# Out-projection of both FFNs as a separate stage of seven Strassen passes over all hidden blocks

## The reference, cut to what matters

```
hf = modulate(rmsnorm(x, norm_w[l, 2]), sh2, sc2)
gate, up = split(hf @ ffn_w_in[l], 2)            # 1024 x 5632
y  = (silu(gate) * up) @ ffn_w_out[l]            # 2816 x 1024, the out-projection
x  = x + g2 * rmsnorm(y, norm_w[l, 3])
```

## Time and profile before

| | |
|---|---|
| runs | 2746.82, 2747.04, 2750.24 us; median 2747.04 |
| profiled execution | 2749.15 us, span 2747.4 us, mean granted clock 0.983 |
| TensorE busy | 2629.4 us, 96%, 12848 matmuls |
| weight loads | 2195.4 us, 80% |
| VectorE | 1691.7 us, 62% |
| GpSimd | 1152.2 us, 42% |
| ScalarE | 966.5 us, 35% |
| DMA | 269 MB, 98 GB/s on average |

### The profile page before, as it was taken

One profiled execution on the slowest core, in us unless ns is written; L12 is line 12 of the kernel. 1 busy time (PEld: TensorE's weight loads), 2 busy tenths in 40 slices (PEclk: granted clock), 3 DMA queues, 4 the chain that ended last, 5 costly groups with the idle time before them and its releaser, 6 DMA issues.

```text
span 2747.4 us, 36296 instructions
## 1 busy us (share of the span) xinstructions
PE 2629.4 (96%) x12848; PEld 2195.4 (80%) x12848; DVE 1691.7 (62%) x2376; ACT 966.5 (35%) x1856; POOL 1152.2 (42%) x788
## 2 busy tenths in 40 slices
PE   7999999999989889999999998999999999999998
PEld 6888788878878678888888877888787888888886
DVE  5378778667756475666656565666436555554556
ACT  5334434443443653233222344111154232223323
POOL 3112332342230036666555641444305665556662
PEclk9999999999999999999999999999999999999999
DMA  6222422432261332112211132332514111111113
GB/s 247 85 70 100 169 108 77 154 128 80 100 227 65 130 123 75 63 62 90 71 61 61 54 139 107 108 107 107 201 52 138 47 59 62 48 46 46 61 46 146
DMA packets 76132, 269.07 MB, mean 98 GB/s; under 512 B 8688, under 2 KB 8688, under 8 KB 72944
## 3 DMA queue, kind: packets, MB, share of 16 engines
q1 hardware_dynamic: 76016, 267.53, 27.1%
HBM read 217.16 MB, written 50.33 MB: 97 GB/s over the span
## 4 chain that ended last, share of the span: by engine, by line
PE 84%; DVE 7%; issue 3%; POOL 3%; ACT 2%; DMA 1%; SPq 0%; POOLq 0%; DVEq 0%; ACTq 0%
PE psum L1189 18%; PE psum L1190 17%; PE psum L1191 17%; PE psum L1720 5%; PE psum L1722 5%; PE psum L1721 5%; PE psum L1386 2%; PE psum L1431 2%; PE psum L1433 2%; PE psum L1432 2%; PE psum L1226 1%; PE psum L1373 1%; PE psum L1246 1%; DVE ada_acc L2581 1%; DVE c_set L2413 1%
## 5 line engine op out<-in xcount | busy, mean ns | idle before, releaser
L1189 PE MATMUL psum<-x_hi,unit 128*128 128x512 f32 x1232 | 484.2, 393 | 5.8 <-DVE x_lo L2413 5.4
L1190 PE MATMUL psum<-x_lo,unit 128*128 128x512 f32 x1232 | 481.5, 391 | 0.0
L1191 PE MATMUL psum<-x_hi,unit 128*128 128x512 f32 x1232 | 481.2, 391 | 0.0
L2413 DVE TENSOR_TENSOR c_set<-c_set,psum 128x512 f32<-128x512 f32 x352 | 233.7, 685 | 354.4 <-PE psum L1191 187.3
L1106 POOL TENSOR_TENSOR unit_sum<-ffn_raw 128x512 f32<-128x512 f32 x200 | 268.2, 1341 | 391.1 <-PE psum L1189 230.2
L2413 DVE TENSOR_TENSOR y<-y,psum 128x512 f32<-128x512 f32 x288 | 193.8, 686 | 159.1 <-PE psum L1722 154.7
L1189 PEld LDWEIGHTS psum<-x_hi,unit 128*128 128x128 f32 x1232 | 232.4, 189 | 61.1 <-ACT c_set L1834 6.2
L1111 POOL TENSOR_TENSOR unit<-unit_sum,unit 128x512 fp32r<-128x512 f32 x200 | 257.6, 1297 | 55.8 <-ACT unit L1834 55.5
L1191 PEld LDWEIGHTS psum<-x_hi,unit 128*128 128x128 f32 x1232 | 232.4, 189 | 48.7
L1190 PEld LDWEIGHTS psum<-x_lo,unit 128*128 128x128 f32 x1232 | 232.4, 189 | 47.6
L1189 PE MATMUL psum<-h_hi,w_hi 128*128 128x512 f32 x624 | 266.3, 427 | 1.3 <-DVE h_lo L2413 1.3
(11 more groups left out here) (303 smaller groups left out, 5290.8 us busy)
## 6 DMA issues: line engine op xcount, KB each, us to landing
ffn_raw<-in_w_ffn_in SPq DMA_DIRECT2D x80, 512.0 KB, 3.5
ffn_raw<-in_w_ffn_out SPq DMA_DIRECT2D x44, 512.0 KB, 4.1
w_raw<-in_w_hgrn_in SPq DMA_DIRECT2D x40, 512.0 KB, 4.7
ada_raw<-in_ada SPq DMA_DIRECT2D x32, 512.0 KB, 3.5
conv_ada_raw<-in_ada SPq DMA_DIRECT2D x32, 512.0 KB, 4.7
units_kept<-stage_unit SPq DMA_DIRECT2D x28, 512.0 KB, 6.1
unit<-units_kept SPq DMA_DIRECT2D x28, 512.0 KB, 4.9
rows_kept<-stage_row SPq DMA_DIRECT2D x12, 1024.0 KB, 8.4
```

The lines of the kernel that those rows point to most:

```text
L1189: begin = pe.matmul(out_ap, hi[:, a:b], rhs_hi, start=first, stop=False)
L1190: pe.matmul(out_ap, hi[:, a:b], rhs_lo, start=False, stop=False)
L1191: return begin, pe.matmul(out_ap, lo[:, a:b], rhs_hi, start=False, stop=last)
L2413: V.tensor_tensor(dst, a, b, op).then_inc(S[sem], 1)
```

## The change

Both FFNs are ordered anew.

- The in-projection runs through all 22 pairs without a matmul of the out-projection between them. `hidden_part` now only multiplies, into one of four fp32 blocks `hid`. VectorE forms five sums of each group's two blocks (`part_sum`, into `part_sums`); SP stores them and two plain halves as seven 128x512 blocks per group in a DRAM tensor `parts_kept` (`parts_store`).
- The low parts of M4 and M3 are made on VectorE (`unit_low`) in place of GpSimd. `ffn_raw` has four slots of one row each.
- The out-projection is a stage after the last pair (`out_products`): seven passes in the order M5, M1, M4, M7, M3, M2, M6, each over the 11 groups, 77 steps. A step loads one kept block (ring of six), splits it (ScalarE `part_high`, VectorE `part_low`), makes the row unit from rows of `ffn_w_out` that lie in SBUF (GpSimd `rows_total` in five passes, ScalarE `row_high`, low part on GpSimd, in these passes on VectorE in every second step), and multiplies: 4 token blocks x 3 matmuls, each token block in a bank of its own that collects the whole pass. Units are in rings of four: what is made for a step may begin when the step three before it has begun.
- After a pass VectorE adds its four banks to the parts of `y` that need them (`out_evac`, 48 operations per FFN), two per step, in steps 3 to 6 of the next pass.
- The last four steps of the last pass run token block by token block. Token blocks 0 to 3 are final after the pass M3; their norms, scalings and turns (8 of 16) are put beside the last two passes, those of blocks 4 to 7 follow the last steps. In the first FFN two convolution panels are loaded and split during the stage.

```
-GROUP_UNITS = 2 * PRODUCTS + 4
+PAIR_UNITS = PRODUCTS * PAIRS
+OUT_KINDS = (M5, M1, M4, M7, M3, M2, M6)
+ROWS_SUMMED = (M1, M4, M7, M3, M6)
+STEPS = PRODUCTS * FFN_GROUPS
+TAIL_GROUPS = 4
+PART_RING, UNIT_RING = 6, 4
...
 # VectorE
-                    tt(up, up, gate, ALU.mult, "hidden_done")
-                    dve.wait_ge(S["hidden_done"], done)
-                    V.tensor_copy(hi[:, cols], up).then_inc(S["hidden_hi_done"], 1)
-                    dve.wait_ge(S["hidden_hi_done"], done)
-                    tt(lo[:, cols], up, hi[:, cols], ALU.subtract, "hidden_ready")
+                    if h is not None:
+                        dve.wait_ge(S["parts_stored"], h * GROUP_STORED + GROUP_STORED * (FFN_GROUPS * f - 1))
+                    tt(hid[e % 4][:, cols_of(half)], up, gate, ALU.mult, "hidden_done")
+                def part_sum(g, k1, j):
+                    dve.wait_ge(S["hidden_done"], g * 4 + (2 * PAIRS * f + 4))
+                    if not (isinstance(g, int) and g + f == 0):
+                        dve.wait_ge(S["parts_stored"], g * GROUP_STORED + GROUP_STORED * FFN_GROUPS * f)
+                    one, other, op = part_terms(OUT_SUMS[j], k1, (k1 + 1) % 4)
+                    tt(part_sums[:, j, :], one, other, op, "part_summed")
...
+                for n in range(2, STEPS):
+                    part_low(n)
+                    if low_by_vector(n):
+                        rows_low(n)
+                    for j in range(len(OUT_SUMS)):
+                        if n == 2 + j // 2:
+                            part_sum(FFN_GROUPS - 1, 0, j)
+                    ...
+                    for m in range(len(EVACS)):
+                        if evac_position(m) == n:
+                            out_evac(m)
+                    if n in EARLY_SCALE:
+                        out_scale_of(EARLY_SCALE[n])
...
 # SyncE, end of the in-projection
+                last_started(M3)
+                for n in range(PART_RING):
+                    part_load(n)
+                last_started(M1)
+                for g in range(4, 8):
+                    out_row_load(1, g, f"row_loaded{g - 4}")
+                last_started(M7)
+                for g in range(8, FFN_GROUPS):
+                    out_row_load(1, g, f"row_loaded{g - 4}")
+                parts_store(FFN_GROUPS - 2, 2)
+                last_started(M6)
+                for n in (PART_RING, PART_RING + 1):
+                    part_load(n)
+                for g in range(4, 8):
+                    out_row_load(0, g, "rows_middle")
+                part_load(PART_RING + 2)
+                part_load(PART_RING + 3)
+                parts_store(FFN_GROUPS - 1, 0)
+                part_load(FFN_GROUPS - 1)
...
 # GpSimd
+                def rows_total(n):
+                    pool.wait_ge(S["out_started"], STEPS * f + n - 2)
+                    ...
+                for n in range(STEPS):
+                    if n + 1 < STEPS and step_kind(n + 1) in ROWS_SUMMED:
+                        rows_total(n + 1)
+                    if not low_by_vector(n):
+                        rows_low(n)
+                    if f == 0 and n in (57, 61):
+                        ...
+                        split_to(N_CONV + j, j, conv_first[j], 1)
...
 # TensorE
+                def step_products(n, tb):
+                    p, g = n // FFN_GROUPS, n % FFN_GROUPS
+                    (of_hi, of_lo, _), (hi, lo, _) = part_unit(n), row_unit(n)
+                    tokens, dst = slice(tb * P, (tb + 1) * P), bank(out_bank(p, tb))
+                    begin = pe.matmul(dst, of_hi[:, tokens], hi[:, :], start=g == 0, stop=False)
+                    pe.matmul(dst, of_hi[:, tokens], lo[:, :], start=False, stop=False)
+                    return begin, pe.matmul(dst, of_lo[:, tokens], hi[:, :], start=False, stop=g == FFN_GROUPS - 1)
+                def out_products():
+                    for n in range(TAIL):
+                        if n % FFN_GROUPS == 0:
+                            bank_free(n // FFN_GROUPS)
+                        if f == 0 and n >= FIRST_TURN:
+                            early_turn(n - FIRST_TURN)
+                        step_ready(n)
+                        for tb in range(4):
+                            begin, mm = step_products(n, tb)
+                            ...
+                    for tb in range(4):
+                        if f == 0 and tb < 3:
+                            early_turn(TAIL - FIRST_TURN + tb)
+                        for n in range(TAIL, STEPS):
+                            if tb == 0:
+                                step_ready(n)
+                            begin, mm = step_products(n, tb)
+                            ...
...
 # TensorE, first convolution panels
-                turns_at = {(0, 1): 8, (0, 3): 9, (0, 5): 10, (0, 7): 11, (1, 4): 12, (1, 6): 13, (2, 0): 14, (2, 2): 15}
+                turns_at = {(0, 7): 8, (1, 1): 9, (1, 3): 10, (1, 5): 11, (2, 0): 12, (2, 2): 13, (2, 4): 14, (2, 6): 15}
```

More of the change, by code:

```diff
@@ L963, in _ @@
             ffn_loads(1, w_ffn_in[1], w_ffn_out[1])
-            for tb in range(LAT):
-                sp.wait_ge(S["x_updated"], 3 * LAT + tb + 1)
-                sp.dma_start(out[tb], xt_end[1][:, tb, :]).then_inc(S["stored"], 16)
             sp.wait_ge(S["stored"], 16 * LAT)
@@ new lines, in ffn_units, with pair_units @@
+                total(2, 2, 0)
+                def pair_units(u, h, e, last=False):
+                    for l in range(PRODUCTS):
+                        if l + 1 < PRODUCTS and l + 1 in SUMMED:
+                            total(u, e, l + 1)
+                        elif l + 1 == PRODUCTS and not last:
+                            raws_ready(h + e % 2, e + 1)
+                            total(u + 1, e + 1, 0)
+                        if l in SUMMED:
+                            low(u, e, l)
@@ L1712, in pair @@
                     for l in range(PRODUCTS):
                         readers_done(u, l)
-                        product(k + l, (slot + l) % 4, l, (b + l) % 4)
-                def partial_products(dst, unit, block, tb, first, last):
-                    hi, lo = unit[:2]
-                    tokens = slice(tb * P, (tb + 1) * P)
-                    of_hi, of_lo = hidden_of(block)
-                    begin = pe.matmul(dst, of_hi[:, tokens], hi[:, :], start=first, stop=False)
-                    pe.matmul(dst, of_hi[:, tokens], lo[:, :], start=False, stop=False)
-                    return begin, pe.matmul(dst, of_lo[:, tokens], hi[:, :], start=False, stop=last)
@@ L1800, in ffn @@
-                k = FFN_UNITS - GROUP_UNITS - 4
-                for nth in range(2):
-                    pair(PAIRS - 2 + nth, k + PRODUCTS * nth, PRODUCTS * nth % 4, PRODUCTS * nth % 4)
-                last_out_group(k + 2 * PRODUCTS)
+                for u in (2, 3):
+                    pair(u, u)
+                with pe.Fori(0, (PAIRS - 6) // 4) as i:
+                    for e in range(4):
+                        pair(i * 4 + (4 + e), e)
+                    if f == 0:
+                        ada_sums(i + G_FFN)
@@ new lines, in ffn @@
+                for l in range(2):
+                    unit_high(f, 2, 1, 2, l)
+                gate_out(1, 0)
+                for u in (2, 3):
+                    pair(u, 1, u)
+                with act.Fori(0, (PAIRS - 6) // 4) as i:
+                    for e in range(4):
+                        pair(i * 4 + (4 + e), i * 2 + (2 + e // 2), e)
+                pair(PAIRS - 2, PAIRS // 2 - 1, 0)
+                out_row_copy(sub)
+                pair(PAIRS - 1, PAIRS // 2 - 1, 1, last=True)
@@ new lines, in ffn @@
+                if f == 1:
+                    for tb in LATE:
+                        out_norm(tb)
+                    return
+                turned(2, 5)
+                out_norm(4)
+                turned(2, 6)
+                out_norm(5)
+                turned(2, 7)
+                end_norm(4)
+                out_norm(6)
+                end_norm(5)
+                out_norm(7)
+                end_norm(6)
+                turned(2, 8)
+                end_norm(7)
+                for t in range(9, 12):
+                    turned(2, t)
@@ new lines, in ffn, with out_evac @@
+                for e in range(2):
+                    pair(PAIRS - 2 + e, PAIRS // 2 - 1, e, FFN_GROUPS - 2, last=e == 1)
+                def out_evac(n):
+                    p, tb, half, c, how = EVACS[n]
+                    src, dst = bank(out_bank(p, tb)), y_of(f, 4 * half + tb, cols_of(c))
+                    dve.wait_ge(S["out_pass"], OUT_FULL * f + p + 1 + (tb if p == LAST_PASS else 0))
+                    if how == COPY:
+                        V.tensor_copy(dst, src).then_inc(S["out_evac"], 1)
+                    elif how == NEGATE:
+                        V.tensor_scalar(dst, src, -1.0, None, ALU.mult).then_inc(S["out_evac"], 1)
+                    else:
```

(14 more changed lines are left out.)

782 lines of the change are left out of this document (408 added, 374 removed), and 4 rows, old and new, of the table out_raws.

## The result

The changed kernel takes 2699.26 us as the median of its first four runs, against 2746.93 for the kernel before in the same session: a ratio of 0.9823, 95% interval 0.9806 to 0.984. The forecast was 2678, range 2670 to 2695: the direction is right, the time is 21 us too low and outside the range. The profiled execution took 2697.19 us (span 2695.5), 52.0 us less than the profiled one of before; forecast were 68.6.

The account below looks back on a forecast made before the run. TensorE's matmul count was taken as the bound: 59.8 us from removed matmuls plus 12.6 at the edge after the first FFN, less 3.8 at the kernel's end, made 68.6 us off; forecast median 2678 us, range 2670 to 2695.

Parts of the forecast that it names:

- rival 3: Where pairs meet the out stage: DRAM round trip not covered, 8 us in place of 2.1, twice; 2690; chance 0.12.
- rival 2: Out stage: shared VectorE-GpSimd port held for whole instructions binds five passes in both FFNs; 27 us, 2705; chance 0.09.
- Matmuls removed: Out-projection: 1056 matmuls become 924 per FFN; 264 fewer at 0.2266 us take off 59.8 us.
- The loop of pairs, the steady passes: In-projection pairs and out-stage passes: moved VectorE and GpSimd work fits, so no TensorE wait; 0 taken for both.
- The last four steps: End of each out stage: four steps ready within 2.04 us, their preparation needs 4.1; loss 2.1 us per FFN.
- End of the kernel: After the second FFN's last product: the end comes 10.9 us later, against 9.1 before; 3.8 us lost with joining and last steps.
- the early norms of blocks 0 to 3: Beside the sixth and seventh passes: norms and turns taken at no cost; only 0.5 us for a weight split.
- Rival 5: Out stage: each VectorE difference lets a whole GpSimd operation pass; costs 74 us, 2752, slower; chance 0.04.
- Joining: Last pair to first out steps: group 9's store lands 7.3 us after the pair, delaying step 3; 2.1 us per FFN.
- ninth turn: Edge after the first FFN: TensorE waits for block 5's diagonal, late on VectorE; 1.0 us.
- No granted clock under 1.0: Sign between first FFN and convolution: TensorE's clock no longer falls; about 3.4 us of such loss counted before.
- The edge before: Old kernel, first FFN's in-projection end through six convolution products: 18.3 of 109.15 us overhead; 5.7 after, gain 12.6.

Follow-up runs that it names:

- The repeated profile: Profile of the changed kernel run again without any edit, as base of the other runs; median 2696.58 us, ratio 0.9805 to the kernel before.
- The three edits: Changed kernel plus group 9's store ahead of row loads, sixth pass's evacuations one step earlier, block 5's diagonal ahead of block 6's scaling; 2681.47 us, ratio 0.9757.
- store first: Changed kernel with SP issuing the store of group 9's parts ahead of the seven weight row loads in both FFNs; 2688.05 us, ratio 0.979.

## Why the prediction was wrong

The measured time is none of the five cases: it lies between the 2690 of rival 3 and the 2705 of rival 2, and neither mechanism is what the traces show. The two out stages, forecast at some 212 us, took 236.2 (6.5 of it for eight turns) and 221.1.

**Matmuls removed: right.** 924 per FFN at an unchanged pitch; the 59.8 us are there. **The loop of pairs, the steady passes: right**, 100.00 of 100 us. **The last four steps: right**, 2.3 and 2.5 us for 2.1. **End of the kernel: right**, 10.15 us to the span's end from the last product for 10.9.

**The step that failed: the early norms of blocks 0 to 3 at nothing.** The prediction let them "lie beside the sixth and seventh" passes, and priced only a weight split of 0.5 us. Measured are 7.1 us in the first FFN and 3.6 in the second. The port's hold was worked out for a pass without them: 5.13 of 5.44 us per two steps. The sixth pass has no sums, hence room; but around it and the start of the seventh stand eight wide operations, in the first FFN also four diagonals and two weight splits of 5.1 and 5.6 us (forecast as one of 4.3), and none of the VectorE work was held against that room. With the scalings and updates narrow, both stalls go; with GpSimd's differences narrow, 3.1 of 3.6 and 3.7 of 7.1 go; with the splits moved, 2.9 of 7.1. So it is VectorE's work stretched by the exclusion at the port. Rival 5's mechanism, an operation of VectorE that lets one of GpSimd pass, costs time there; in the steady passes it is seen as well, in differences of up to 1.8 us instead of 0.69, and is covered.

**Joining: the mechanism right, the size too small.** 2.1 us per FFN forecast, 3.9 and 3.5 as stalls. The store landed 10.0 us after the pair, not 7.3. I had SP issue it on time and the engines at full rate; SP was busy with seven issues of 0.57 us until 1405.5, and more loads entered behind. (The sum itself was a little off: 5.5 MB at 0.41 MB/us from 10.9 us on are through 5.3 us after the pair, not 6.) Rival 3's long round trip with no cover is not it: a change of order removes the stall of step 3 and leaves 1.5 us at step 10.

**The granted clock: left out.** In the first profile the mean clock over the 10 us behind both joins, the first early turn and the ninth turn is 0.83 to 0.85, about 1.7 us each, which brings the joins to 5.6 and 5.2 us. The repeated profile has it behind the first join and the ninth turn only, so part of this cost is chance. The prediction had this cost in the kernel before and left it out after, on "No granted clock under 1.0".

**The two turns.** The first early turn's 2.4 us were not seen: its evacuation stands one step too late in VectorE's program. The ninth was named, at 1.0, and measured 2.6 and the clock.

**The sum.** Joins 6.6 more than forecast, middles 10.2, early turn 4.5, ninth turn about 3.5: 25 us. Some 8 to 9 came back that I had not counted. The traces name about that much. The edge before was 19.6 us, not 18.3: the sixth convolution product's last matmul starts at 1717.36, so my stretch ended 1.3 us short. And the loops of before were not without waits. Counted from the starts of the matmuls (distances more than 0.05 us over the pitch), they lost 4.9 us in the first FFN (1002 to 1606) and 2.6 in the second (2092 to 2689), in gaps of 0.1 to 0.7 us, in the first FFN about half of it at the starts of output groups; the loops of pairs after lost 0.4 and 0.1. That is 7.0 us which the change saved and I had put at nothing, because the earlier trace rows shows the time in flight, in which a gap of 0.1 us vanishes. Besides, the granted clock at the start of the second FFN fell for about twice as long before as after, some 1.5 us, which is chance. Together these make a little more than what came back; executions differ by more than the rest. The three edits that act on joins and turns bring 2681.5, with the port's share still in it; that is inside the range, and 3.5 us over the forecast.

## What to carry to other kernels

Work that is moved "beside" another stage must be added to that stage's scarcest resource, here the port that VectorE and GpSimd share, not to each engine's idle time: the steady passes ran without a stall with the two at 77 and 79%, which left less room than it seemed, and in the middle VectorE was busy 21.68 of 22 us and late. When a store and loads share one queue, ask for the store that someone waits for first; and when the engines of DMA are full, expect a reordering to move part of a stall and not only to end it. Price a wait of TensorE of 2.7 us or more at a joint with about 1.7 us on top for its clock (21 of 22 such stalls at the joins and the ninth turn had it); at 2.4 to 2.5 us it came in 10 of 18 cases.

## What the runs showed of the hardware

A diagonal of 128x128 on VectorE takes 0.29 us alone and 1.1 beside GpSimd, so what an operation loses at the port does not shrink with its size: small ones lose most in proportion. The same stall lowers the granted clock in one execution and not in the next: 2.4 us ahead of the first turn brought 0.85 over 10 us in the first profile of the changed kernel and left it at 1.00 in the second, and 2.5 us at step 63 left it at 1.00 in both, while in "store first" it brought 0.83. The part before the first FFN, the same in all changed kernels, took between 968 and 979 us in different executions, more than most of the effects studied here, so single effects are read from a stretch of the trace, not from the medians.
